# A two-layer transformer pair on one core: the cross attentions' query product by Strassen's algorithm

## What is computed

```python
def memory_cross_attention(h, mem_n, w_q, w_kv, w_o):
    bsz, s, _ = h.shape
    m = mem_n.shape[1]
    q = (h @ w_q).reshape(bsz, s, X_HEADS, X_HEAD_DIM)
    k, v = jnp.split(mem_n @ w_kv, 2, axis=-1)
    k = k.reshape(bsz, m, X_HEADS, X_HEAD_DIM)
    v = v.reshape(bsz, m, X_HEADS, X_HEAD_DIM)
    logits = jnp.einsum('bshd,bmhd->bhsm', q, k).astype(jnp.float32) * (X_HEAD_DIM ** -0.5)
    p = jax.nn.softmax(logits, axis=-1)
    o = jnp.einsum('bhsm,bmhd->bshd', p.astype(v.dtype), v)
    return o.reshape(bsz, s, D_MODEL) @ w_o
```

## Time and profile before

| | us |
|---|---|
| median of 3 runs | 3568.8 |
| lowest and highest run | 3568.12, 3573.12 |
| the profiled execution | 3571.2 |
| its span, first to last instruction | 3569.3 |
| TensorE busy | 3363.8 (94%) |
| VectorE busy | 2152.7 (60%) |
| ScalarE busy | 1437.0 (40%) |
| GpSimd busy | 158.4 (4%) |

### The profile page before, as it was taken

One profiled execution on the slowest core, in us unless ns is written; L12 is line 12 of the kernel. 1 busy time (PEld: TensorE's weight loads), 2 busy tenths in 40 slices (PEclk: granted clock), 3 DMA queues, 4 the chain that ended last, 5 costly groups with the idle time before them and its releaser, 6 DMA issues. The chain is left out here.

```text
span 3569.3 us, 58080 instructions
## 1 busy us (share of the span) xinstructions
PE 3363.8 (94%) x23652; PEld 2850.4 (80%) x23652; DVE 2152.7 (60%) x3108; ACT 1437.0 (40%) x2312; POOL 158.4 (4%) x214
## 2 busy tenths in 40 slices
PE   7789899999999899999999989999999999999997
PEld 5687787888878587888877778788888767878886
DVE  5636553777744753677767454587763555358775
ACT  5323243533333743443334233443332574344332
POOL 0110000000000000000000200000000251000000
PEclk9899899999999999999999899999999999999998
DMA  3002131222231031222221023222231102212221
GB/s 146 25 4 99 71 130 48 94 95 94 107 109 71 33 122 64 80 105 106 94 86 66 3 93 109 71 95 94 94 134 65 37 2 95 107 71 95 94 94 47
DMA packets 42735, 289.92 MB, mean 81 GB/s; under 512 B 5475, under 2 KB 6243, under 8 KB 8860
## 3 DMA queue, kind: packets, MB, share of 16 engines
q1 hardware_dynamic: 42524, 286.92, 21.8%
HBM read 284.79 MB, written 2.12 MB: 80 GB/s over the span
## 5 line engine op out<-in xcount | busy, mean ns | idle before, releaser
L308 DVE TENSOR_TENSOR w_lo<-w_raw,w_hi 128x2048 fp32r<-128x2048 f32 x145 | 330.1, 2277 | 332.5 <-ACT w_hi L300 332.2
L1340 PE MATMUL ps<-mlp_u_hi,w_lo 128*128 128x512 f32 x1024 | 404.6, 395 | 0.0
L1339 PE MATMUL ps<-mlp_u_lo,w_hi 128*128 128x512 f32 x1024 | 404.5, 395 | 0.0
L1338 PE MATMUL ps<-mlp_u_hi,w_hi 128*128 128x512 f32 x1024 | 404.5, 395 | 0.0
L1077 ACT ACTIVATE w_hi<-w_raw 128x1024 fp32r<-128x1024 f32 x168 | 171.5, 1053 | 424.8 <-PE ps L1340 386.1
L414 PE MATMUL ps<-x_hi,w_hi 128*128 128x512 f32 x768 | 309.9, 404 | 23.9 <-PEq L270 16.3
L300 ACT ACTIVATE w_hi<-w_raw 128x2048 fp32r<-128x2048 f32 x145 | 274.8, 1895 | 121.3 <-PE ps L1340 68.6
L414 PE MATMUL ps<-x_hi,w_lo 128*128 128x512 f32 x768 | 307.5, 400 | 0.0
L414 PE MATMUL ps<-x_lo,w_hi 128*128 128x512 f32 x768 | 307.4, 400 | 0.0
L1188 DVE TENSOR_TENSOR hT<-hT,ps 128x512 f32<-128x512 f32 x256 | 170.6, 683 | 186.3 <-PE ps L1340 186.3
L1319 PE MATMUL ps<-a_x_hi,w_hi 128*128 128x256 f32 x896 | 253.6, 283 | 8.4 <-DVE mlp_sum L1174 8.4
(11 more groups left out here) (605 smaller groups left out, 7746.8 us busy)
## 6 DMA issues: line engine op xcount, KB each, us to landing
w_raw<-in_weights SPq DMA_DIRECT2D x255, 1024.0 KB, 4.8
x_mem<-in_mem SPq DMA_DIRECT2D x4, 1024.0 KB, 4.9
hT<-in_x SPq DMA_DIRECT2D x1, 2048.0 KB
d_bias<-bias_rows SPq DMA_DIRECT2D x1, 2048.0 KB, 8.0
n_w<-in_cmp_w SPq DMA_DIRECT2D x1, 2048.0 KB, 7.4
out_h<-hT SPq DMA_DIRECT2D x1, 2048.0 KB, 6.3
t_xi<-in_ret_xi SPq DMA_DIRECT2D x1, 1024.0 KB, 7.2
w_raw<-in_weights SPq DMA_DIRECT2D x2, 512.0 KB, 3.3
```

What stands on the lines that cost most here:

```text
L308: dve.tensor_tensor(self.wlo[b % SPLIT][:, 0:width], self.raw[b % RAW][:, 0:width], self.whi[b % SPLIT][:, 0:width].bitcast(F32), ALU.subt ...
L1338: pe.matmul(c.ps[:, 4 + i, :], whi[:, k, cols], u_hi[g % 2][:, k, :], start=k == 0, stop=False)
L1339: pe.matmul(c.ps[:, 4 + i, :], whi[:, k, cols], u_lo[g % 2][:, k, :], start=False, stop=False)
L1340: mm = pe.matmul(c.ps[:, 4 + i, :], wlo[:, k, cols], u_hi[g % 2][:, k, :], start=False, stop=k == 3)
```

## The change

The queries' product is no longer a `linear` but a new stage, `linear_by_quarters`. Weights and tokens are each seen as 2x2 quarters: the weights of two blocks (512 output columns) as a11, a12 (first block), a21, a22 (second block), the tokens as b11, b12, b21, b22 by upper or lower half of the features and first or second half of the tokens. Seven products of mixed quarters give the four corners of the result. With 1024 output columns there are two such units, so 14 products of 24 matmuls with 256 columns. For each unit VectorE makes four mixes of weights (1024 elements in each partition), five lower parts of mixed or moved quarters and seven additions of products into sums and corners; ScalarE makes the five upper parts and copies the first product. The two units use different halves of PSUM. The factor 1/16 on the queries moves to the copy of the keys.

The norm beside the keys' product becomes `QuarterNorm`. It has the squares in two steps of four, the roots at block 2 and the spreading at block 3. VectorE multiplies four tiles at block 3 and four at block 4, and makes four mixes of the tokens' quarters (t1 to t4, at blocks 4 and 5). ScalarE makes the upper part of seven operands, and VectorE of all seven the lower part (blocks 3 to 7), each of 1024 elements in a partition. GpSimd has no part in it. The new buffers `q_t_hi` and `q_t_lo` hold three of the mixed operands.

```diff
+class QuarterNorm(Norm):
+        self.order = ["b11", "b21", "b22", "t1", "t3", "t2", "t4"]
...
+    def plan(self):
+        halves = (range(0, 4), range(4, 8))
+        pe = {2: self.sums, 3: self.spread_roots}
+        act = {0: partial(self.squares, halves[0]), 1: partial(self.squares, halves[1]), 2: self.roots.root, 3: partial(self.hi_quarters, (0,)),
+               4: partial(self.hi_quarters, (1, 2)), 5: partial(self.hi_quarters, (3, 4)), 6: partial(self.hi_quarters, (5, 6))}
+        dve = {0: partial(self.add_squares, halves[0]), 1: partial(self.add_squares, halves[1]), 2: self.roots.refine, 3: self.first_tiles,
+               4: self.second_tiles, 5: self.mix_tokens, 6: partial(self.lo_quarters, (3, 4)), 7: partial(self.lo_quarters, (5, 6))}
+        return pe, act, dve
...
+    def hi_quarters(self, which, act):
+        for n in which:
+            if n < 3:
+                act.wait_ge(self.normed.sem, self.normed.at((4, 8, 8)[n]))
+            else:
+                act.wait_ge(self.made.sem, self.made.at(n - 2))
+            act.activation(self.places[n][1], self.places[n][0], ACT.Copy).then_inc(self.parts_hi.sem, self.parts_hi.up())
...
+def linear_by_quarters(c, sb, name, operands, out):
+    steps = [(0, 0, "b11"), (0, 1, "b21"), (1, 0, "t2"), (1, 1, "t3"), (0, 0, "t4"), (1, 0, "t1"), (1, 1, "b22")]
...
+            first_mixes(0)
+            for n in range(units):
+                a11, a12, _, _, _ = factors(n)
+                if n == 0:
+                    mix(n, 2, a11, s1[n], a11, ALU.subtract)
+                step_part(n, 2)
+                mix(n, 3, a12, a12, a11, ALU.subtract)
+                step_part(n, 3)
+                step_part(n, 4)
+                dve.wait_ge(copied.sem, copied.at(n + 1))
+                add(n, corner(n, 0), first_product, 1)
+                if n:
+                    dve.wait_ge(added.sem, added.at(7 * n))
+                add(n, sums[0], first_product, 2)
+                step_part(n, 5)
+                add(n, sums[1], sums[0], 3, 2)
+                step_part(n, 6)
+                add(n, corner(n, 1), sums[1], 4, 3)
+                if n + 1 < units:
+                    first_mixes(n + 1)
+                following = tops[n] + 2
+                if following < len(c.blocks):
+                    c.make_lo(dve, following, c.blocks[following][2])
+                if n + 1 < units:
+                    mix(n + 1, 2, factors(n + 1)[0], s1[n + 1], factors(n + 1)[0], ALU.subtract)
+                add(n, corner(n, 2), sums[1], 5)
+                add(n, sums[2], sums[0], 5)
+                add(n, corner(n, 3), sums[2], 6, 6)
...
-            ins = act.activation(kT[:, t, :], psum[:, 0:M], ACT.Copy)
+            ins = act.activation(kT[:, t, :], psum[:, 0:M], ACT.Copy, scale=1 / 16)
...
+    qT = y
     with c.memory() as sb2:
-        linear(c, name + "_kv", m_hi, m_lo, M, ["T"] * 4 + ["N"] * 4, act_evac=kv_evac,
-               side=Norm(c, c.hT, T, weight, x_hi, x_lo, sb2("norm_buf", [P, KD, T]), sb2("norm_col", [P, 5, NT])))
-    qT = y
-    linear(c, name + "_q", x_hi, x_lo, T, ["T"] * 4, act_evac=tile_evac(qT, 1 / 16))
+        t_hi, t_lo = ([sb2(f"q_t_{part}{i}", [P, 4, HT], F32R)[:, :, :] for i in range(3)] for part in ("hi", "lo"))
+        with c.memory() as sb3:
+            quarters = QuarterNorm(c, weight, x_hi, x_lo, t_hi, t_lo, sb3("norm_buf", [P, KD, T]), sb3("norm_col", [P, 5, NT]))
+            linear(c, name + "_kv", m_hi, m_lo, M, ["T"] * 4 + ["N"] * 4, act_evac=kv_evac, side=quarters)
+        with c.memory() as sb3:
+            linear_by_quarters(c, sb3, name + "_q", quarters.operands, qT)
```

More of the change, by code:

```diff
@@ L352, in linear @@
     pe_side, act_side, dve_side = {}, {}, {}
-    if side:
+    if side and side.plan:
+        side.start()
+        pe_side, act_side, dve_side = side.plan()
+    elif side:
         side.start()
@@ L642 @@
 class Norm:
-    POOL = 3
+    POOL, plan = 3, None
     def __init__(self, c, src, n_tok, weight, out_hi, out_lo, buf, col, source=None, row=None, ahead=None):
```

150 lines of the change are left out of this document (added).

## The result

| | before | after |
|---|---|---|
| median of the runs | 3569.2 us (20 runs, 3564.0 to 3581.9) | 3576.6 us (20 runs, 3570.9 to 3582.9) |
| profiled execution, its span | 3571.2 us, 3569.3 us | 3572.7 us, 3570.8 us |

The ratio of after to before is 1.0018, with a 95% interval of 1.001 to 1.0026. By the ratio the change costs 6.4 us (3.6 to 9.3), by the two medians 7.4 us, which is about the 0.2% that a measurement can tell. The forecast was 3567 us with a range up to 3576 us: the sign is wrong, and the time lies just above the range, where rival C stood. The two profiled executions are only 1.5 us apart, so most of the loss is not in this pair of traces.

What follows compares the result with a forecast made beforehand. TensorE alone was taken to bound the queries' product. Per cross attention, +5.5 us keys' stage, -7.2 queries' stage and +1.2 for slow stretches leave -0.5, so -2 in all: 3567 us from 3568.8, range 3558 to 3576.

Steps and rivals of the forecast that it cites:

- rival C: Both slow stretches show in each cross attention: +1.3 us each, +5 us in all, so slower; chance 0.13.
- Keys' stage: Keys' product with the norm beside it: stalls stretch it from 52.1 to 57.7 us, taken as plus 5.5.
- one behind the first is free: Keys' stage: a slow stretch after the 2.8 us idle time costs nothing, since TensorE waits for weights later anyhow.
- the price of one behind the second: Keys' stage: a slow stretch after the 3.3 us idle time delays block 6's evacuations and the barrier by up to 1.5 us.
- Queries' stage: Queries' product by quarters: 40.3 us at full clock against 47.5, minus 7.2 us a cross attention.
- Rival D: Narrow matmuls go at their weight loads' pace, 0.191 us each: 98 us more in all, 3666 us; chance 0.01.
- the rule on narrow matmuls: Queries' product: a 256-column matmul costs at least 0.62 of a 512-column one, so 48.5 us against 44.8, a loss.
- Rival B: Keys' stage doesn't stretch, as VectorE's 43 us fit into 52: 3540 us in full, mild form to 3559; chance 0.22.
- The clock: Slow stretches after TensorE's idle times in both stages: 0 to 3.0 us shown per cross attention, 1.2 taken, against 1.5 before.
- each pays this once: Queries' stage before: each of four cross attentions loses about 1.5 us to one slow stretch.
- The one long idle time that is followed by a slow stretch is 2.38 us: Ahead of the queries' product before: slow stretches follow this idle time, but not those of 0.71 and 1.13 us.
- the full-clock part: Both stages at full clock: +5.5 - 7.2 = -1.7 us a cross attention, but 1.5 us before were a slow stretch.

Runs made afterwards that it cites:

- the new order: Changed kernel with the side work beside the keys' product reordered: 3561.0 us with four lower parts on GpSimd, 3555.8 us with all seven on VectorE.
- the second trace: The kernel before run once more, unchanged, for a second trace: 3570.2 us, ratio 0.9996.
- after_again: The changed kernel run once more, unchanged, for a second trace: 3575.1 us, ratio 1.0017.

## Why the prediction was right or wrong

- **Keys' stage: right.** Forecast 57.7 us, measured 57.8, 58.1, 59.4 and 57.7. The instruction chain held almost to a tenth in the first cross attention. The first multiplication was to start 25.9 us from the stage's start and did at 25.87; block 5's, 6's and 7's lower parts were to end at 33.9, 42.8 and 50.4 and ended at 33.9, 42.8 and 50.3; VectorE's last part at 57.4 and did at 57.5. The stalls were 1.1, 2.5, 1.4 and 1.7 us against 1.5, 2.8, 3.3 and 2.0. The third was short because the slow stretch behind the second fell into it. In the third cross attention none did, and that stall was 2.95 us, near the forecast; a slow stretch came behind it instead, and that stage took 59.4 us, 1.3 to 1.7 us more than the others. So "one behind the first is free" and the price of one behind the second were right too.
- **Queries' stage: right.** Forecast 40.3, measured 40.7, 41.6, 41.9 and 41.0; in the first 6.2 us stand ahead of the third product (forecast 6.3) and 1.28 us at the end (1.2). Rival D and the rule on narrow matmuls are out: 24 of 256 columns took 2.72 us again in the first cross attention. In the second they took 2.83 us, at full clock, which makes its stage 41.6 us. I have no reason for that.
- **Rival B: out as it stood, and right in another way.** VectorE's 43 us do fit into 52, as the new order shows, but not in the order of the change.
- **The clock: the step that failed.** "The shown price is so between 0 and 3.0 us; I take 1.2", less the 1.5 us of before, was worked out for the two stages alone. There the stages sum to -2.2 us in the first pair of traces, as forecast, but to -0.3 us in the mean of two pairs. Two assumptions in it were wrong. First, "each pays this once" took the slow stretch of before as fixed because it came four times in four; in the second trace it came in two of four, so before is cheaper than the sum's base. Second, the term ended at the scores. Of 8 MLPs each in the two traces, those of after have a slow stretch at their start in 8 (2 before) and at their second idle place in 2 (4 before): two stretches, 3 us, more in an execution. "The one long idle time that is followed by a slow stretch is 2.38 us" left these places out: the trace it was read from has 2.58 us of idle TensorE at the MLP's start without a stretch in four of four, and 2.11 us 38 us later with one in two of four. The term that was to be -0.3 us a cross attention, 1.2 less 1.5, was in truth some +2.2 by the means (20 us more at half clock, 0.43 x 20 = 8.8 us in all), wherever in the kernel they lie. With the full-clock part, where -0.2 each was forecast and -0.7 measured at equal slow time, this makes +6 instead of -2. Rival C's time was right; its mechanism, both slow stretches in each cross attention, shows in one of four in each trace of after.
- What remains open: why the MLP's start, with the same 2.58 us of idle TensorE ahead of it, is followed by a slow stretch 8 times in 8 after, and 2 in 8 before. The runs show that it is so, that it goes with the queries' product and not with the norm (20 in 28 against 2 in 12), and what one costs. They don't show what in the timing upstream decides it, nor where the rest of the 20 us lies.
- **The range.** Its upper end, +7, was worked out from the two stages alone; by its own terms (1.3 + 0.6) x 4 is 7.6. The measured +6.4 of the ratio lies inside it with an interval that reaches beyond (3.6 to 9.3), and the median came half a microsecond above the range.

## What to carry to other kernels

Follow an added chain instruction by instruction through the order in which each engine takes them: that foretold each stall here to within half a microsecond where no slow stretch fell into it, while the sum of busy times (43 of 52 us) foretold none, and the same work in another order left the stage at its old length. A stage's price doesn't end with the stage: count each idle time of TensorE in the whole kernel that is as long as one that a slow stretch followed anywhere. Take how often that happens, and not only how dear it is, from more than one execution. Compare two kernels at equal granted clock before explaining a difference of 0.2%, and see first whether the two traces differ by it at all. Cheap matmuls whose result nobody reads were worth 0.3 to 0.4% in an idle time of 5.4 us in each cross attention, and cost their full time where TensorE was not idle.

## What the runs showed of the hardware

- **VectorE beside GpSimd.** Two mixes of 1024 elements on VectorE (float32, both inputs in SBUF) took 2.48 us alone and 6.79 us while GpSimd worked on two subtractions of the same kind. Those took 6.08 us, where one alone takes 2.73. Together they lasted from 506.84 to 514.00, 7.2 us, against 7.9 for one after the other: little of it overlapped. The Trainium skill, "SBUF — State Buffer", section "SBUF: two separate sides", says that a VectorE operation with two SBUF inputs and a GpSimd operation that reads SBUF take the same pair of ports, and whichever comes second is blocked for the whole instruction. The trace agrees, nearly: 6.79 us is 2.48 plus 4.3, somewhat less than two of GpSimd's.
- **Slow stretches and chance.** The same program with the same idle times (2.4 us ahead of the queries' product) had the slow stretch in four of four places in one execution and in two of four in another. An idle time of 2.58 us at one place had it in 2 of 12 cases in kernels with one product upstream, and in 20 of 28 with the other. One of 1.86 us, too, was followed by it (in after_again, 51.1 us into the first keys' stage). The mean granted clock of single runs of before went from 0.966 to 0.978, and the time with it from 3598 to 3556 us.
- **The price is steady.** A stretch of 3.4 us costs 1.5 us in each place where nothing waits anyhow, and over all runs of the two kernels it is 0.43 us for each us at half clock, not 0.5. The 1.5 of 3.4 us is the same share, 0.44: in such a stretch the starts were 0.43 us apart, less than twice 0.233.
